# The raw weights of the experts: a ring of twelve places in place of four

## What is computed

```python
def moe_swiglu(h, w_router, w_gu_e, w_dn_e):
    logits = (h @ w_router).astype(jnp.float32)          # 256 x 8
    top_val, top_idx = lax.top_k(logits, TOP_K)          # 2 of 8 experts a token
    top_w = jax.nn.softmax(top_val, axis=-1)
    combine = jnp.sum(jax.nn.one_hot(top_idx, N_EXPERTS) * top_w[..., None], axis=-2)
    for e in range(N_EXPERTS):                           # w_gu_e[e]: 1024 x 2816, w_dn_e[e]: 1408 x 1024
        out = out + combine[..., e:e + 1] * swiglu(h, w_gu_e[e], w_dn_e[e])
```

## Time and profile before

| | |
|---|---|
| median of three runs | 3361.84 us |
| the profiled execution, its own time | 3365.45 us |
| its span, first to last instruction | 3363.7 us |
| PE busy | 3066.9 us (91%) |
| DVE busy | 1804.5 us (54%) |
| ACT busy | 1494.0 us (44%) |
| read from HBM | 441.43 MB, 132 GB/s over the span |
| granted clock of TensorE, mean | 0.950 of full speed |

### The profile page before, as it was taken

How to read it: one execution, slowest core, us unless ns; L and a number is a source line. 1 busy time by engine, 2 the same in 40 slices (tenths; PEclk the granted TensorE clock), 3 DMA queues, 4 the chain that set the end, 5 groups by cost and what they waited for, 6 DMA issues and landing times. The chain is left out here.

```text
span 3363.7 us, 40588 instructions
## 1 busy us (share of the span) xinstructions
PE 3066.9 (91%) x14628; PEld 2308.8 (69%) x14628; DVE 1804.5 (54%) x2562; ACT 1494.0 (44%) x2269; POOL 43.7 (1%) x50
## 2 busy tenths in 40 slices
PE   6998998997999999788999999699997998999798
PEld 5667887665666666566776667477775676766797
DVE  4545674645777777422453433564663424544676
ACT  4535564534566665422334332553442423443554
POOL 0000000000000000000000100000000010000000
PEclk9999999998999999788999999799998988999899
DMA  5325785323888887211230212253551222322364
GB/s 179 118 89 181 244 272 154 114 93 115 259 264 271 266 265 240 76 57 32 70 90 32 66 38 76 66 172 119 148 162 42 82 71 84 91 85 85 113 182 125
DMA packets 352361, 444.79 MB, mean 132 GB/s; under 512 B 19536, under 2 KB 197840, under 8 KB 352192
## 3 DMA queue, kind: packets, MB, share of 16 engines
q1 hardware_dynamic: 349488, 434.40, 41.8%
q0 software_dynamic: 2144, 6.74, 0.6%
q10 hardware_dynamic: 560, 1.41, 0.1%
HBM read 441.43 MB, written 1.05 MB: 132 GB/s over the span
## 5 line engine op out<-in xcount | busy, mean ns | idle before, releaser
L1262 DVE TENSOR_TENSOR w_lo<-raw,w_hi 128x1024 fp32r<-128x1024 f32 (+1 forms) x866 | 1010.3, 1175 | 928.2 <-ACT w_hi L897 813.7
L897 ACT ACTIVATE w_hi<-raw 128x1024 fp32r<-128x1024 f32 (+1 forms) x866 | 873.0, 1016 | 541.4 <-PE ps L1881 141.5
L1909 PE MATMUL ps<-w_hi,h_hi 128*128 128x512 f32 (+1 forms) x1008 | 423.7, 422 | 19.0 <-DVE h_lo L1564 16.6
L1909 PE MATMUL ps<-w_hi,h_lo 128*128 128x512 f32 (+1 forms) x1008 | 395.3, 394 | 0.0
L1868 PE MATMUL ps<-h_hi,w_hi 128*128 128x256 f32 (+1 forms) x1056 | 316.7, 325 | 21.0 <-issue 14.9
L1868 PE MATMUL ps<-h_lo,w_hi 128*128 128x256 f32 (+1 forms) x1056 | 313.9, 322 | 0.0
L1922 PE MATMUL ps<-w_lo,h_hi 128*128 128x512 f32 (+1 forms) x1008 | 308.7, 391 | 0.0
L1909 PEld LDWEIGHTS ps<-w_hi,h_hi 128*128 128x128 f32 x1008 | 197.2, 196 | 82.8 <-issue 33.1
L1868 PEld LDWEIGHTS ps<-h_hi,w_hi 128*128 128x128 f32 x1056 | 203.7, 193 | 50.1 <-issue 16.5
L1881 PE MATMUL ps<-w_hi,act_hi 128*128 128x512 f32 x528 | 217.6, 412 | 11.8 <-ACT w_hi L897 11.8
L1137 ACT ACTIVATE arena<-ps,att 128x512 f32<-128x512 f32 (+2 forms) x128 | 72.8, 569 | 331.9 <-DVE att L1637 321.3
(11 more groups left out here) (259 smaller groups left out, 4319.4 us busy)
## 6 DMA issues: line engine op xcount, KB each, us to landing
raw<-in_w_in SPq DMA_DIRECT2D x196, 512.0 KB, 3.6
raw<-in_w_gu_exp SPq DMA_DIRECT2D x128, 512.0 KB, 4.7
raw<-in_w_mod SPq DMA_DIRECT2D x96, 512.0 KB, 4.6
raw<-in_w_up SPq DMA_DIRECT2D x88, 512.0 KB, 4.0
raw<-in_w_dn_exp SPq DMA_DIRECT2D x80, 512.0 KB, 4.9
raw<-in_w_gu_exp SPq DMA_DIRECT2D x64, 384.0 KB, 3.9
raw<-in_w_gu_dense SPq DMA_DIRECT2D x44, 512.0 KB, 5.0
raw<-in_w_down SPq DMA_DIRECT2D x40, 512.0 KB, 3.7
```

The source lines that it names most:

```text
L897: nc.scalar.activation(w_hi[:, half, 0:n], raw[:, slot, 0:n], ACT.Copy).then_inc(seg.sig.hi_ready, 1)
L1262: nc.vector.tensor_tensor(w_lo[:, half, 0:n], raw[:, slot, 0:n], w_hi[:, half, 0:n].bitcast(F32), ALU.subtract).then_inc(seg.sig.lo_ready, 1)
L1909: ins = mm(ps[:, 2 * h + p % 2, 0:width], x[:, k + c, p * P:(p + 1) * P], wh[:, c * width:(c + 1) * width], start=opens and c == 0 and x i ...
```

## The change

The experts' raw units go to a ring of DEEP = 12 places. Eight are new: four at 8192 to 12287 of the arena and four at 14720 to 18815, both unused in that stage. The other four are the places of `raw`. Each of the twelve has a semaphore of its own. The load of unit j now waits for DVE to be done with unit j - 12. Since the arena is in use earlier, SP also waits, once ahead of the first expert load, for the barrier behind `norm` (`deep_free`). The expert units no longer count in the rotation of `raw`: a separate count, `load`, goes on from the router's units to the next segment. Sizes of loads, their number, their order, and all that ACT, DVE and PE compute are unchanged.

```diff
@@ -48,6 +48,8 @@
 AHEAD = 2
 RAW, HL = 4, 3
 
+DEEP = 3 * RAW
+
 QK_SB, V_SB, QK_FX, V_FX, F_FX, G_1 = 0, 1024, 1536, 2560, 3072, 3080
 
 MQ, MK, MV, MO, MG, AQ, NQ, NK, NV, G_2 = 0, 512, 1024, 1536, 2048, 2064, 2832, 3344, 3856, 4368
@@ -125,6 +127,9 @@
         self.dt, self.after, self.gate0, self.y_pairs, self.y_turned = dt, after, gate0, y_pairs, y_turned
         self.looped = iters > 2
         assert not self.looped or self.n % RAW == 0 and self.n % HL == 0
+
+        self.load0, self.deep = at["load"], mode == "moe" and half == 0
+        assert not self.deep or self.n % DEEP == 0
         self.results = max(u[0] for u in units) + 1
         self.next, self.first = None, False
         self.alone = mode == "moe"
@@ -173,8 +178,18 @@
     def loaded(self, it, j):
 
         if self.looped:
-            return it * (16 * self.n // RAW) + 16 * ((self.unit0 + j) // RAW)
-        return 16 * ((self.unit0 + it * self.n + j) // RAW)
+            return it * (16 * self.n // RAW) + 16 * ((self.load0 + j) // RAW)
+        return 16 * ((self.load0 + it * self.n + j) // RAW)
+
+    def place(self, it, j, m, width, raw, deep, deep_loaded):
+
+        if not self.deep:
+            i = (self.load0 + j + (0 if self.looped else it * self.n)) % RAW
+            return raw[:, i, 0:m * width], self.sig.raw_loaded[i], self.loaded(it, j)
+        i = j % DEEP
+        near = i - (DEEP - RAW)
+        slot = deep[i] if near < 0 else raw[:, (self.load0 + near) % RAW, :]
+        return slot[:, 0:m * width], deep_loaded[i], it * (16 * self.n // DEEP) + 16 * (j // DEEP + 1)
 
 
 class Step:
@@ -275,9 +290,12 @@
         prob_t = view(PROB_AT + 1024, 2, 512)
         turn_value = view(Y_AT, 2, 512)
 
+        deep = [view(at + i * UNIT, UNIT) for at in (QKV_AT, 13312 + FE) for i in range((DEEP - RAW) // 2)]
+
 
         main, over = Stream(sem, ""), Stream(sem, "over_")
         experts_main, experts_over = Experts(sem, "moe_"), Experts(sem, "over_moe_")
+        deep_loaded = [sem(f"deep_loaded_{i}") for i in range(DEEP)]
         params_loaded = sem("params_loaded")
         later_loaded = sem("later_loaded")
         cond_hi_done = sem("cond_hi_done")
@@ -325,7 +343,7 @@
         stored = sem("stored")
 
 
-        START = {"unit": RAW, "result": 2, "turn": 4, "item": 2, "pair": 2, "ml": 2}
+        START = {"unit": RAW, "load": RAW, "result": 2, "turn": 4, "item": 2, "pair": 2, "ml": 2}
         STARTS = [(x, n) for st in (main, over) for x, n in ((st.hi_ready, RAW), (st.lo_ready, RAW), (st.hi_used, RAW),
                                                              (st.units_used, RAW), (st.results_saved, 2))]
         STARTS += [(x, M) for e in (experts_main, experts_over) for x in e.all]
@@ -353,7 +371,7 @@
             s.turned = dict(halves)
             halves.clear()
             s.sig, s.unit0, s.result0 = main, count["unit"], count["result"]
-            took(unit=s.n * iters)
+            took(unit=s.n * iters, load=0 if s.deep else s.n * iters)
             if not s.paced:
                 took(result=s.results * iters)
             else:
@@ -381,7 +399,7 @@
         def add_overflow(mode, units, iters, flag, evac=None, **kw):
 
             s = Segment(units, iters, mode, dict(count), evac, **kw)
-            s.sig, s.unit0, s.result0 = over, START["unit"], START["result"]
+            s.sig, s.unit0, s.load0, s.result0 = over, START["unit"], START["load"], START["result"]
             s.first = s.alone = True
             s.flag, s.before, s.ready = flag, segments[-1], count["d"]
             segments.append(s)
@@ -612,6 +630,7 @@
             under = [branch(a["w_o_fox"][l], dt, TT, y_fx, g_fx, gates_fx[dt], 1, y_pairs=count["pair"]) for dt in range(2)]
             mixed_out(a["w_out"][l], TT, under[1], evac="residual")
             norm(TT)
+            deep_free = count["barrier"]
             turn_tokens(XN, TT, lambda t: cols[:, col_first(l, "g_ffn"):][:, 0:DC], None)
             if l % 2:
                 logits = view(2048, 2, 512)[0:N_EXP, 0, 0:T]
@@ -631,7 +650,7 @@
                     kw = dict(A=(h_hi[:, :, T:T + P], h_lo[:, :, T:T + P]), N=P, tiles=1, evac="experts", route=route, down=DOWN,
                               ex=ex, half=half, buf=buf, scale=cols[:, col_first(l, "g_ffn"):][:, 0:DC])
                     if half == 0:
-                        add_segment("moe", units, N_EXP, **kw)
+                        add_segment("moe", units, N_EXP, **kw).deep_free = deep_free
                     else:
                         add_overflow("moe", units, N_EXP, buf["flag"], **kw)
                     meet()
@@ -803,12 +822,13 @@
             def load(seg, it, j):
                 q, k, m, opens, closes, width, source = seg.units[j]
 
-                sp.wait_ge(seg.sig.lo_ready, seg.unit(it, j) - RAW + 1)
-                slot = seg.slot(it, j, RAW)
-                dst = raw[:, slot, 0:m * width].rearrange("p (c n) -> p c n", c=m)
-                sp.dma_start(dst, source(it)).then_inc(seg.sig.raw_loaded[slot], 16)
+                sp.wait_ge(seg.sig.lo_ready, seg.unit(it, j) - (DEEP if seg.deep else RAW) + 1)
+                dst, loaded, n = seg.place(it, j, m, width, raw, deep, deep_loaded)
+                sp.dma_start(dst.rearrange("p (c n) -> p c n", c=m), source(it)).then_inc(loaded, 16)
 
             def loads(seg):
+                if seg.deep:
+                    sp.wait_ge(at_barrier, 4 * seg.deep_free)
                 if seg.iters > 2:
                     with sp.Fori(0, seg.iters) as it:
                         for j in range(seg.n):
@@ -890,11 +910,12 @@
             def split(seg, it, j):
                 q, k, m, opens, closes, width, source = seg.units[j]
                 n = m * width
-                slot, half = seg.slot(it, j, RAW), seg.slot(it, j, HL)
-                act.wait_ge(seg.sig.raw_loaded[slot], seg.loaded(it, j))
+                half = seg.slot(it, j, HL)
+                src, loaded, at = seg.place(it, j, m, width, raw, deep, deep_loaded)
+                act.wait_ge(loaded, at)
                 act.wait_ge(seg.sig.hi_used, seg.unit(it, j) - HL + 1)
                 act.wait_ge(seg.sig.lo_ready, seg.unit(it, j) - HL + 1)
-                nc.scalar.activation(w_hi[:, half, 0:n], raw[:, slot, 0:n], ACT.Copy).then_inc(seg.sig.hi_ready, 1)
+                nc.scalar.activation(w_hi[:, half, 0:n], src, ACT.Copy).then_inc(seg.sig.hi_ready, 1)
 
             def save(seg, it, j):
 
@@ -1258,8 +1279,9 @@
                 n = m * width
                 dve.wait_ge(seg.sig.hi_ready, seg.unit(it, j) + 1)
                 dve.wait_ge(seg.sig.units_used, seg.unit(it, j) - HL + 1)
-                slot, half = seg.slot(it, j, RAW), seg.slot(it, j, HL)
-                nc.vector.tensor_tensor(w_lo[:, half, 0:n], raw[:, slot, 0:n], w_hi[:, half, 0:n].bitcast(F32),
+                half = seg.slot(it, j, HL)
+                src, loaded, at = seg.place(it, j, m, width, raw, deep, deep_loaded)
+                nc.vector.tensor_tensor(w_lo[:, half, 0:n], src, w_hi[:, half, 0:n].bitcast(F32),
                                         ALU.subtract).then_inc(seg.sig.lo_ready, 1)
 
             def save(seg, it, j):
```

## The result

The kernel after takes 3280.48 us (median of four runs, 3277.64 to 3284.0), the kernel before 3361.05 us beside it: a ratio of 0.9762 (95% interval 0.9745 to 0.9779), 80.6 us faster. The forecast was 3307 us, in a range from 3275 to 3333: the right sign and inside the range, 5 us above its lower end, but with 55 us of gain where there were 81. The rival "the engines' own floor is reached", at 3285 us, came nearest.

A forecast was written before the change was run, and what follows sets the result against it. The prediction took the turn of four load places to bound units 8 to 23 of each expert. Savings of 47 us there and 8 us in the other units, less 0 to 1 for the start, gave 55 us: 3307 us, range 3275 to 3333.

The forecast's parts named there:

- the engines' own floor is reached: Rival for the expert stage: DVE's 21.4 us and PE's 34 us are reached, 77 us saved, 3285 us; chance 0.20.
- The bound: Expert stage, units 8 to 23: four places, each held 6.8 us, pass one unit per 1.70 us.
- Units 8 to 23: These units of each expert fall from 28.2 to 22.3 us, 47 us saved over eight experts.
- DVE's floor of 21.4 us: Units 8 to 23: 19.99 us busy plus 0.06 us for each of 23 instructions on DVE.
- Unit 24 to unit 7: From unit 24 to the next expert's unit 7: 37.1 us becomes 36.0, 8 us saved in seven times.
- the sign that PE's work was judged wrongly there: Unit 24 to the next expert's unit 7: its 37.1 us change by more than 3 us either way.
- The transfers: Expert loads: the DMA engines can carry the 297 GB/s needed, with 8% to spare of an estimated 322.
- rival of a DMA bound: Expert stage: the rate ends at 275 to 290 GB/s, saving 45 to 20 us, say 3328 us; chance 0.14.
- The barrier and the start: Ahead of the first expert load: SP's wait for the barrier behind norm costs 0, at most 2 us.
- even sharing among the twelve loads: Stage start, upper bound not taken: the first load lands only with the twelfth, 20 us later; router's result 14 us late.
- The metric of PE: Expert stage: by PE's busy time only 31 us could be gained, 3331 us; by matmul starts 55 us.
- The 1 MiB rule: Expert loads of 512 KB: by the skill's rule more places would not help; cited for no change, 3362 us, chance 0.04.

The follow-up runs named there:

- run with less on PE: The kernel after without the expert units' hi by lo matmuls, a third of the stage's unit matmuls: 3241.88 us, ratio 0.9627 to the kernel before.
- run of before with less on PE: The kernel before without the expert units' hi by lo matmuls: 3360.18 us, ratio 0.9994.

## Why the prediction was right, and where it was short

- **The bound: right for units 8 to 23, and wider than I had it.** It was the turn of the places, there and, as the third point says, in the others too. Four places, wherever they lie, give the time of before; six bring most; nine all.
- **Units 8 to 23, mis-sized.** Predicted 22.3 us, measured 20.16. The step that failed is DVE's floor of 21.4 us, which I made from its busy time and 0.06 us behind every instruction; 0.9 us more went on top for the fixed order of the engines, and were not needed either. The run with less on PE has DVE at 18.6 us. Its instructions overlap when they follow each other at once (timeline of DVE, kernel after):

```profile
1001.14 4.10 DVE L1284 TENSOR_TENSOR w_lo<-arena,w_hi 128x1024 fp32r<-128x1024 f32 x4 [0.50 <-ACT w_hi L918]
...
1005.76 1.82 DVE L1284 TENSOR_TENSOR w_lo<-arena,w_hi 128x768 fp32r<-128x768 f32 x2
```

  The four are units 14 to 17, two of 1.22 us and two of 0.95: 4.34 us one by one, 4.10 as they ran; the two of 768 take 1.82, not 1.90. The 2.24 us of the earlier trace rows were one case in which the second came a little late (ACT ended its part for it at 1042.26 us, DVE began at 1042.28), and I made a rule of it. That such instructions overlap in a profile the Trainium skill says too ("Perfetto Trace Analysis", Optimizing Scalar/DVE Operations: part of a profiled instruction, the acknowledgement of its write, lies beside the next one), and these rows agree: some 0.08 us at each of the four joints. PE's own count, 20.5 us from the starts, was right to 0.3 us, and PE was the bound. This term is 2.1 us an expert, some 17 us in all.
- **Unit 24 to unit 7, mis-read.** Predicted 36.0 us, measured 34.11, which was the lower bound of the text (34 us, from the same starts). I took the time of before for PE's, because PE was busy 36.3 of 37.1 us, although the text itself said that this busy time hides gaps. I also took 36.3 us for the windows at a granted clock of 1.00; they took 36.3 to 37.5 us, so dips of the clock were not the main thing there. The run of before with less on PE shows that PE did not set it: 36.4 us with a third of the matmuls gone. The change of 3.03 us is just over the 3 us that the prediction named as the sign that PE's work was judged wrongly there. 1.9 us an expert, 13 us in all. With the other term's 17 us that makes some 30 us, the difference between the 55 us of the sum and the stage's 85.0.
- **The transfers: right, and with more room.** Needed were 319 GB/s, not 297, and they came without a wait. The estimate of 322 GB/s at full share was too low: the run with less on PE has 343 to 357 over 80 us. The rival of a DMA bound was further off than its 0.14 said.
- **The barrier and the start: right,** cost 0; no even sharing among the twelve loads was seen, since ACT could take the first one 5.8 us after its issue and not 20.
- **Slices.** The stretch of high traffic starts in the eleventh slice of the earlier trace rows, not the tenth (115 GB/s); nothing hangs on that.
- **How far it was luck.** The time fell inside the range, but both terms were too small in the same direction, and what came lies below all that the text called the engines' own floor (3285 us). The ring as the cause is shown; the size of the gain was not foreseen.
- **The metric of PE.** By matmul busy time the gain would have ended at 31 us. The Trainium skill ("Trainium Kernel Development and Optimization", Performance Expectations) sets LDWEIGHTS busy above it. The runs agree: in units 8 to 23 it went from 16.8 of 28.2 us to 18.15 of 20.16, from 59% to 90%, while matmul busy went from 89% to 100%. In the other units, where matmul busy already stood at 98%, it went from 73% to 79% (26.81 of 34.11 us) with PE the bound.
- **The 1 MiB rule.** In the first burst, with up to twelve loads of 512 KB queued, windows of the kernel after show:

```profile
798.00:808.00 10.00, 2.26 (x12) 2.17 (x12) 4.98 (x27) 1.86 (x3) 0.00 (x0) 0.63 1.05 390
790.00:800.00 10.00, 7.13 (x36) 4.67 (x34) 8.27 (x17) 4.79 (x7) 0.00 (x0) 0.64 1.01 366
```

  So loads of 512 KB have 366 to 390 GB/s once several are queued. The rule of the Trainium skill ("DMA: Bandwidth & Descriptors", Bandwidth: transfers of at least 1 MiB for three quarters of the peak), as I had read it against the change, did not hold here.

## What to carry to other kernels

A ring of places is held for landing plus every engine that still reads the place; divide that turn by the places and compare it with what the last engine needs for a unit, taken from the starts of its instructions when they follow each other, not from their busy time. Add places until the quotient is safely below, here six for most and nine for all, and look for them in memory that the stage leaves unused. Before that, check that the wait for loads is handed on down the chain: in the dense stage it was 43 us long, and taking it away brought no gain that the runs can show.

## What had not been expected of the hardware

- An engine's busy time fell when it was fed without gaps: DVE's 23 instructions in units 8 to 23 covered 19.99 us in the kernel before and 18.62 us in the kernel after, with the same durations of one (1.22 us).
- Landing hardly rose with the depth: 4.6 us median and 7.2 at most with four places; with twelve, 5.3 and 7.6 us into the arena and 4.6 and 7.4 us into raw (871.8 to 1251.9 us), while the rate went from 267 to 319 GB/s.
- The DMA engines' busy share is no fixed measure of their rate: at shares of 0.99 to 1.05 they carried 343 to 390 GB/s.
